# A two-layer trunk on one core: V product and last down product with tokens stationary, opening in halves, attention by token parity

## The chip, the core and the metric

The kernel runs on one core of one Trainium2 chip. The time is device microseconds of one execution, the median of several. Five engines work beside each other and meet at semaphores: TensorE (PE, with its weight loads listed apart as PEld), VectorE (DVE), ScalarE (ACT), GpSimd (POOL), and SyncE (SP), which here only issues DMAs.

## The reference

```python
# x: (1, 256, 2048) float32. Layer 0 mixes by gMLP, layer 1 by dilated attention; each is followed by a conv FFN.
h = h + gmlp_chunk_mixer(rms_norm(h, a_ln), ...)      # z = gelu(h W_in); u, v = split(z); v = layer_norm(v)
                                                      # mixed = tril(w_s) v per 128-token chunk + b_s; (u * mixed) W_out
h = h + conv_ffn(rms_norm(h, ffn_ln[0]), ...)         # (silu(dwconv3(h W_gate)) * (h W_up)) W_down, FFN_DIM 5632
h = h + dilated_attention_mixer(rms_norm(h, b_ln), ...)  # 3 groups x 8 heads, (window, dilation) = (128,1) (512,4) (2048,16)
h = h + conv_ffn(rms_norm(h, ffn_ln[1]), ...)
return rms_norm(h, final_ln)
```

With 256 tokens every window reaches back to the start, or nearly so: a query sees the keys of its group whose distance is no more than the window and a multiple of the dilation. For dilations 4 and 16 these have the parity of the query.

## The kernel before

Activations lie with features on the partitions: a tile of 128 features by 256 tokens. `h` is the residual (16 such tiles). Float32 accuracy comes out of float32r products by splitting: a weight tile W becomes `w_hi` (ACT copies `raw` and rounds) and `w_lo` (DVE subtracts), an activation becomes a high part and a low part that lie side by side in `X`, `GX`, `OX` or `hid` as 512 columns. For each 128 by 128 weight tile PE loads `w_hi`, streams the 512 columns, loads `w_lo` and streams the 256 high columns (`multiply`, L1054). The sum lands in two halves of a PSUM bank, which ACT and DVE add when they empty it.

All weights come as one stream of 784 units of 8 tiles (512 KB each). SP loads unit u into `raw[u % 4]` as soon as `w_lo` of unit u-4 is made (L341 on); ACT's and DVE's `split_step` (L439, L744) run two units ahead of the step they stand in; ACT may overwrite a slot when PE has finished the unit four back. Everything else that ACT and DVE do is written out by hand between these splits, by step number. The stages: V (units 0 to 31, from 10.41 us), U (32 to 63, from 103.71), AO (the gMLP's output product), F0 and D0 (FFN of layer 0), QKV (eight heads of 18 units, from 1030.64), WO, F1, and D1, the last down product (88 units, from 2011.60 to 2255.66).

What the change touches:

- **Opening.** SP issues `vecs`, then the four first units. ACT issues five loads of `x` (`X_LOADS`, blocks 2, 2, 4, 4, 4) and makes the high parts, DVE the low parts, each pair or four of them followed by one split. PE warms up with 30 matmuls on zeros. Then ACT squares `h` in pairs into `tsum` and `hc` in turn, and POOL adds them into `ssum` (L384); a square may only overwrite a tile that has been added. `mean_square` on PE sums over the partitions after unit 7.
- **V and U, layer norm.** V is emptied pair by pair (`scale_pair` on DVE, Gelu on ACT, L482), POOL sums the pairs into `vsum` (L398). The mean product (L1149) stands after unit 3 of U; then DVE subtracts the mean, ACT squares into U's last tiles, POOL adds eight times (L409), and after unit 10 PE waits for `ln_added` and takes the variance (L1154). From unit 14 on each feature tile is scaled (L925, L928), turned by PE (L1170), copied by ACT, and mixed by PE with `WS` (L1162); DVE adds the bias (`mix_bias`), POOL multiplies into U.
- **Attention.** `scores` (L1193) gives the first 128 queries 128 keys, the second 128 queries 256 keys, in each of three groups: 384 + 768 columns. `p_turn` turns nine 128 by 128 blocks, `attend` has nine products of 128 columns. These float32 products show as two PE instructions each; a turn shows as one.
- **End.** D1 is emptied as the other residual products are; `last_block` takes the last two tiles. Then PE turns `Y` (h times the final gain) to token-major in 32 turns (L1287) with the sum of squares between (L1304), ACT and DVE scale eight 128x512 pieces (L738, L1048), and SP stores them.

## Time and profile before

| | us |
|---|---|
| median of the timed runs | 2267.44 (2267.21 to 2267.46) |
| the profiled execution | 2269.09 |
| its span | 2267.4 |
| PE busy in the span | 2252.1 |
| DVE busy | 1479.9 |
| ACT busy | 1215.5 |
| POOL busy | 105.5 |

Busy time is time in which an engine has an instruction under way. A group of the page gives busy time, the mean duration of one, and the idle time of its engine before it with what ended that. A matmul's duration reaches past the start of the next one, because the array is pipelined; what counts in a stream is the distance from start to start. A timeline row gives a start, the time the row covers, and how many instructions were merged.

### The profile page before, as it was taken

Reading aid. Unit: us, or ns where it says so; the run is one execution under the profiler, and the core shown is the slowest. Engines: PE = TensorE matmul, PEld = TensorE weight load, DVE = VectorE, ACT = ScalarE, POOL = GpSimd, SP = SyncE. Lnnn points to the kernel's source line nnn. Section 1 sums busy time; section 2 is a strip of 40 time slices with the busy share of each in tenths; the row PEclk is TensorE's granted clock in tenths of the full one; section 3 lists DMA queues with packets and bytes.
Section 4 is the critical chain, followed back from the end, with each engine's and each line's share of the span. In section 5 each row is a group of like instructions: output and inputs, shape, how many; then the busy total and the mean of one; then the engine's idle time right before and its main releaser. Section 6 shows DMA issues by size and latency. Waiting matters only on the chain.

```text
span 2267.4 us, 37978 instructions
## 1 busy us (share of the span) xinstructions
PE 2252.1 (99%) x13098; PEld 1998.8 (88%) x13098; DVE 1479.9 (65%) x1764; ACT 1215.5 (54%) x1544; POOL 105.5 (5%) x85
## 2 busy tenths in 40 slices
PE   9999999999999999999999999999999999999998
PEld 7888888888888888888888888888888888888887
DVE  6577776767666655556666666687666666655453
ACT  6455566666666634445555555555555555544443
POOL 3122100000000000000000000020000000000000
PEclk9999999999999999999999999999999999999999
DMA  7645565555555565555555555556555555566564
GB/s 263 197 157 168 178 201 186 192 186 190 189 185 190 190 194 188 191 188 201 168 168 167 171 171 167 172 166 198 187 191 187 190 189 185 190 192 193 186 190 134
DMA packets 115478, 419.22 MB, mean 185 GB/s; under 512 B 12832, under 2 KB 12960, under 8 KB 115168
## 3 DMA queue, kind: packets, MB, share of 16 engines
q1 hardware_dynamic: 114192, 413.43, 56.3%
q0 software_dynamic: 512, 2.95, 0.3%
q10 hardware_dynamic: 720, 2.10, 0.2%
q8 instruction: 37, 0.61, 0.1%
q14 instruction: 17, 0.14, 0.0%
HBM read 416.33 MB, written 2.10 MB: 185 GB/s over the span
## 4 chain that ended last, share of the span: by engine, by line
PE 97%; POOL 1%; DMA 1%; DVE 0%; ACT 0%; issue 0%; ACTq 0%; DVEq 0%; POOLq 0%
PE acc L1063 61%; PE acc L1064 32%; POOL vsum L409 1%; DMA h<-x_t 1%; PE sc_ps L1218 0%; POOL ssum L384 0%; PE sc_ps L1198 0%; PE sc_ps L1205 0%; PE acc L1261 0%; PE sc_ps L1213 0%; PE sc_ps L1197 0%; PE misc L1189 0%; ACT U L618 0%; PE misc L1162 0%; PE sc_ps L1162 0%
## 5 line engine op out<-in xcount | busy, mean ns | idle before, releaser
L1063 PE MATMUL acc<-X,w_hi 128*128 128x512 f32 x4480 | 1564.3, 392 | 3.5 <-DVE w_lo L750 3.0
L750 DVE TENSOR_TENSOR w_lo<-raw,w_hi 128x1024 fp32r<-128x1024 f32 x784 | 967.9, 1241 | 527.5 <-ACT w_hi L446 527.2
L1064 PE MATMUL acc<-X,w_lo 128*128 128x256 f32 x4480 | 1263.3, 282 | 0.0
L446 ACT ACTIVATE w_hi<-raw 128x1024 fp32r<-128x1024 f32 x784 | 824.8, 1058 | 496.2 <-PE acc L1064 486.8
L1063 PEld LDWEIGHTS acc<-X,w_hi 128*128 128x128 f32 x4480 | 841.6, 188 | 179.6 <-DVE w_lo L750 3.6
L1064 PEld LDWEIGHTS acc<-X,w_lo 128*128 128x128 f32 x4480 | 847.2, 189 | 0.4
L1063 PE MATMUL acc<-hid,w_hi 128*128 128x512 f32 x1408 | 488.2, 390 | 0.0
L1064 PE MATMUL acc<-hid,w_lo 128*128 128x256 f32 x1408 | 397.1, 282 | 0.0
L1063 PEld LDWEIGHTS acc<-hid,w_hi 128*128 128x128 f32 x1408 | 264.4, 188 | 55.4
L1064 PEld LDWEIGHTS acc<-hid,w_lo 128*128 128x128 f32 x1408 | 266.1, 189 | 0.0
L456 ACT ACTIVATE hc<-acc 128x512 f32<-128x512 f32 x104 | 62.0, 596 | 157.3 <-PE acc L1064 157.3
L755 DVE TENSOR_TENSOR tsum<-hc,acc 128x512 f32<-128x512 f32 x104 | 71.5, 687 | 97.3 <-ACT hc L456 97.2
L374 POOL TENSOR_TENSOR ssum<-ssum,sq 128x512 f32<-128x512 f32 x24 | 33.0, 1376 | 1271.7 <-ACT sq L459 1271.7
L1063 PE MATMUL acc<-GX,w_hi 128*128 128x512 f32 x256 | 88.9, 391 | 0.0
L516 ACT ACTIVATE conv<-gu,vecs 128x256 f32<-128x256 f32 x88 | 53.1, 603 | 61.2 <-DVE gu L772 61.2
L772 DVE TENSOR_TENSOR gu<-tsum,rinv 128x512 f32<-128x512 f32 x104 | 72.3, 695 | 3.6
L1064 PE MATMUL acc<-GX,w_lo 128*128 128x256 f32 x256 | 72.2, 282 | 0.0
L654 ACT ACTIVATE hc<-acc 128x512 f32<-128x512 f32 (+1 forms) x40 | 22.2, 555 | 81.3 <-PE acc L1064 81.3
L466 ACT ACTIVATE X<-h,vecs (+1 forms) x48 | 22.0, 504 | 72.3 <-DVE h L786 71.9
L1063 PEld LDWEIGHTS acc<-GX,w_hi 128*128 128x128 f32 x256 | 48.0, 188 | 10.1
L766 DVE SCALAR_TENSOR_TENSOR X<-h,vecs,X (+1 forms) x64 | 38.5, 628 | 21.9 <-ACT X L466 17.7
L521 ACT ACTIVATE act_g<-conv 128x256 f32<-128x256 f32 x88 | 36.8, 419 | 26.7 <-DVE conv L801 26.5
(141 smaller groups left out, 1049.0 us busy)
## 6 DMA issues: line engine op xcount, KB each, us to landing
raw<-w_stream SPq DMA_DIRECT2D x784, 512.0 KB, 3.5
out<-out_sb SPq DMA_DIRECT2D x8, 256.0 KB, 2.9
h<-x_t ACTq DMA_DIRECT2D x3, 512.0 KB, 10.3
WS<-ws_t POOLq DMA_DIRECT2D x1, 1024.0 KB, 5.2
BS<-bs_row POOLq DMA_DIRECT2D x1, 1024.0 KB, 8.2
mask<-mask_d POOLq DMA_DIRECT2D x1, 576.0 KB, 4.0
h<-x_t ACTq DMA_DIRECT2D x2, 256.0 KB, 5.0
rope<-rope_d POOLq DMA_DIRECT2D x1, 256.0 KB, 3.2
```

What stands on the lines that cost most here:

```text
L374: nc.gpsimd.tensor_tensor(ssum[:, :], ssum[:, :], sq[:, :, :].rearrange("p a b -> p (a b)"), ALU.add).then_inc(ss_added, 1)
L409: nc.gpsimd.tensor_tensor(vsum[:, :, :], vsum[:, :, :], U[:, 12 + 2 * k:14 + 2 * k, :], ALU.add)\
L446: nc.scalar.activation(w_hi[slot][:, :], raw[slot][:, :], ACT.Copy).then_inc(hi_ready, 1)
L456: nc.scalar.activation(hc[:, :, :], acc[s][:, :, 0:S], ACT.Copy).then_inc(hcopied, 1)
L516: nc.scalar.activation(conv[:, :], gu[:, 0, 2:S + 2], ACT.Identity, bias=vecs[:, one(cv + 3 * FB + j)], scale=vecs[:, one(cv + 2 * FB + j) ...
L521: nc.scalar.activation(act_g[:, :], conv[:, :], ACT.Silu).then_inc(silued, 1)
L750: nc.vector.tensor_tensor(w_lo[slot][:, :], raw[slot][:, :], w_hi[slot][:, :], ALU.subtract)\
L755: nc.vector.tensor_tensor(tsum[:, :, :], hc[:, :, :], acc[s][:, :, S:2 * S], ALU.add)\
L766: nc.vector.scalar_tensor_tensor(X[:, 2 * pr + b, S:2 * S], h[:, 2 * pr + b, :], vecs[:, one(GAINS[n] + 2 * pr + b)], X[:, 2 * pr + b, 0:S ...
L772: nc.vector.tensor_tensor(gu[:, :, 2:S + 2], tsum[:, :, :], over(rinv, 2), ALU.mult)\
L1063: nc.tensor.matmul(bank, hi, moving[:, kt, :], start=first, stop=False)
L1064: op = nc.tensor.matmul(bank[:, S:2 * S], lo, moving[:, kt, 0:S], start=False, stop=last)
```

## The change

The stream, the split and all other stages stay.

- `token_unit` replaces `multiply` in V and D1. A unit is then two k-tiles by 512 output columns. For each k-tile and each half of the tokens PE loads the high part of the activations and streams 512 columns of `w_hi`, loads the low part and streams `w_hi`, loads the high part and streams `w_lo`: twelve matmuls of 512 columns in a unit, one PSUM bank for each 128 tokens.
- V lands token-major. `v_evac` applies the RMS factor and Gelu straight from PSUM and sums along the row; the layer norm's statistics are row sums on ACT (`v_square`) and DVE, its gain and bias come as broadcast rows (two further 1 MB loads on POOL's queue) and are applied by `v_norm`, two DVE instructions of 512 columns, eight times. POOL's sums, the two mean products and the turns of V go. The mixes move from after units 16 to 31 of U to after units 12 to 27. Two one-column products (`tok_ms`) join the first `mean_square`.
- The opening loads, rounds and splits the first unit in halves; `vecs` is loaded behind the first units; the warm-up has 15 matmuls; the split of a step now stands ahead of its two squares.
- Attention has the even tokens ahead of the odd ones. The groups with dilation 4 and 16 need keys of the same parity alone: 1024 score columns, eight turns, and in `attend` two products of 256 columns and four of 128.
- In D1 the last four units are run for the first 128 tokens and then for the others. `h` is turned to token-major beforehand, by 32 turns inside F1 (`h_turn`), so that the end needs none; the final norm's sum of squares is a row sum, the first half of the tokens is finished and stored apart from the second.

The opening loop stands on ACT, `v_norm` on DVE at steps 8 to 15 of U:

```diff
-        sp.dma_start(vecs[:, :], vecs_d).then_inc(vecs_landed, 16)
-        for slot in range(RING):
+        sp.dma_start(raw[0][:, 0:UC // 2], w_stream[0, :, 0:UC // 2]).then_inc(raw_half, 16)
+        sp.dma_start(raw[0][:, UC // 2:UC], w_stream[0, :, UC // 2:UC]).then_inc(raw_landed[0], 16)
+        for slot in range(1, RING):
             load(slot, 0, slot)
+        sp.dma_start(vecs[:, :], vecs_d).then_inc(vecs_landed, 16)
...
+        def token_unit(u, slot, pair_set, moving, k0, k_tiles, needs=None, half=None):
+            if half is None:
+                pe.wait_ge(lo_ready, u + 1)
+            for j in range(2):
...
+                hi, lo = w_hi[slot][:, COLS * j:COLS * (j + 1)], w_lo[slot][:, COLS * j:COLS * (j + 1)]
+                for t in range(2):
+                    bank = acc[pair_set][:, t, :]
+                    xh, xl = moving[:, kt, P * t:P * (t + 1)], moving[:, kt, S + P * t:S + P * (t + 1)]
+                    nc.tensor.matmul(bank, xh, hi, start=(kt == 0), stop=False)
+                    nc.tensor.matmul(bank, xl, hi, start=False, stop=False)
+                    op = nc.tensor.matmul(bank, xh, lo, start=False, stop=(kt == k_tiles - 1))
+            op.then_inc(units_done, 1)
...
-        for n, (tile, cols) in enumerate(((warm_r, 512),) * 16 + ((warm_r, P),) * 8 + ((warm_b, 512),) * 6):
+        for n, (tile, cols) in enumerate(((warm_r, 512),) * 11 + ((warm_r, P),) * 4):
...
+        for s in range(2, BLOCKS * BLOCK_UNITS + 4):
             split_step(U_V, s)
+            if s < 6:
+                for i in (2 * s - 4, 2 * s - 3):
+                    wait_pos(act, ss_added, i - 1)
+                    nc.scalar.activation((tsum, hc)[i % 2][:, :, :], h[:, pair_of(i), :], ACT.Square)\
+                        .then_inc(x_squared, 1)
...
+        def v_norm(c, t):
+            at = V[:, t, COLS * c:COLS * (c + 1)]
+            dve.wait_ge(ln_landed, 32)
+            nc.vector.scalar_tensor_tensor(at, at, v_shift[:, t:t + 1], ln_gain[:, COLS * c:COLS * (c + 1)],
+                                           ALU.add, ALU.mult).then_inc(v_gained, 1)
+            dve.wait_ge(v_gained, 2 * c + t + 1)
+            nc.vector.scalar_tensor_tensor(at, at, v_rinv[:, t:t + 1], ln_bias[:, COLS * c:COLS * (c + 1)],
+                                           ALU.mult, ALU.add).then_inc(v_normed, 1)
```

The lines of the diff on attention and on the end (the first `y_out` is ACT's; `h_turn` is PE's, after each of eight units of F1):

```diff
         def scores(h_, par):
             pe.wait_ge(roped, GROUPS * (h_ + 1))
             for g in range(GROUPS):
-                q, k = QK[par][:, g, 0, :], QK[par][:, g, 1, :]
-                nc.tensor.matmul(sc_flat[:, P * g:P * (g + 1)], q[:, 0:P], k[:, 0:P], start=True, stop=True)
-                op = nc.tensor.matmul(sc_flat[:, Q1 + S * g:Q1 + S * (g + 1)], q[:, P:S], k, start=True, stop=True)
+                for t in range(2):
+                    q = QK[par][:, g, 0, P * t:P * (t + 1)]
+                    a, b = (0, S) if g == 0 else (P * t, P * (t + 1))
+                    c = Q0 * t + (S + P * (g - 1) if g else 0)
+                    op = nc.tensor.matmul(sc_flat[:, c:c + b - a], q, QK[par][:, g, 1, a:b], start=True, stop=True)
...
+        def y_out(t):
+            act.wait_ge(y_biased, 1)
+            act.wait_ge(y_squared, 2 * BLOCKS - 1 + t)
+            nc.scalar.activation(fin_std[:, t:t + 1], y_rows[:, t, BLOCKS - 1:BLOCKS], ACT.Sqrt,
+                                 bias=y_bias[:, t:t + 1], scale=1.0 / D).then_inc(fin_rms[t], 1)
+            act.wait_ge(fin_rinv_ready[t], 1)
+            for c in (1, 2):
+                at = Z[:, t, COLS * c:COLS * (c + 1)]
+                nc.scalar.activation(at, at, ACT.Copy, scale=fin_rinv[:, t:t + 1]).then_inc(y_out_act[t], 1)
...
+        def h_turn(n):
+            wait_pos(pe, h_turned, n - 3)
+            for k in range(4):
+                op = nc.tensor.transpose(turned[n % 4][:, P * k:P * (k + 1)],
+                                         h[:, 2 * n + k // 2, P * (k % 2):P * (k % 2 + 1)], ident[:, :])
+            op.then_inc(h_to_turn, 1)
```

## Rows read from the trace of the kernel before

**Rows 1.** The page: the span and the busy time of each engine.

```profile
span 2267.4 us, 37978 instructions
PE 2252.1 (99%) x13098; PEld 1998.8 (88%) x13098; DVE 1479.9 (65%) x1764; ACT 1215.5 (54%) x1544; POOL 105.5 (5%) x85
```

**Rows 2.** PE's waits over the whole span: engine, line, releaser, us, times, longest.

```profile
PE misc L1154 <- POOL vsum L409: 2.0, 1, 2.0
```

**Rows 3.** Instructions grouped by line and shape: busy us, mean ns, then idle before.

```profile
L750 DVE TENSOR_TENSOR w_lo<-raw,w_hi 128x1024 fp32r<-128x1024 f32 x784 | 967.9, 1241 | 527.5 <-ACT w_hi L446 527.2
...
L446 ACT ACTIVATE w_hi<-raw 128x1024 fp32r<-128x1024 f32 x784 | 824.8, 1058 | 496.2 <-PE acc L1064 486.8 <-DMA raw<-w_stream 5.3 <-PE acc L1262 1.2
```

**Rows 4.** Stretches, one per stage: busy us of each engine, granted clock, DMA share, GB/s.

```profile
10.41:103.71 93.30, 90.34 (x519) 79.56 (x517) 61.81 (x61) 53.66 (x70) 26.45 (x18) 1.00 0.67 230
103.71:208.74 105.03, 102.99 (x619) 91.88 (x617) 78.66 (x105) 55.31 (x77) 31.20 (x18) 0.98 0.49 156
...
1030.64:1472.94 442.30, 442.30 (x2641) 395.14 (x2640) 301.88 (x362) 231.38 (x305) 3.48 (x5) 1.00 0.53 172
...
2011.60:2255.66 244.06, 244.06 (x1411) 216.37 (x1410) 118.56 (x107) 102.61 (x114) 9.82 (x8) 1.00 0.56 177
```

**Rows 5.** PE in order of time, in the last down product: start, duration, what.

```profile
2225.15 0.39 PE L1063 MATMUL acc<-hid,w_hi 128*128 128x512 f32 x1
2225.38 0.28 PE L1064 MATMUL acc<-hid,w_lo 128*128 128x256 f32 x1
2225.50 0.39 PE L1063 MATMUL acc<-hid,w_hi 128*128 128x512 f32 x1
```

**Rows 6.** PE in order of time, in the warm-up: start, duration of the group, count.

```profile
7.77 0.62 PE L1134 MATMUL acc<-warm_r 128*128 128x512 f32 x2
9.29 1.47 PE L1134 MATMUL acc<-warm_b 128*128 128x512 bf16 x6
```

**Rows 7.** PE in order of time, around the second mean product of the U stage.

```profile
137.28 1.98 PE L1154 MATMUL misc<-vsum,mean_w 128*128 128x256 f32 x4 [2.04 <-POOL vsum L409]
```

**Rows 8.** Two single units of the U stage, as stretches.

```profile
196.70:200.14 3.44, 3.44 (x23) 3.12 (x23) 3.36 (x6) 2.56 (x4) 0.00 (x0) 1.00 0.42 138
205.50:208.73 3.23, 3.23 (x23) 2.90 (x22) 1.93 (x4) 0.53 (x2) 2.61 (x2) 1.00 0.53 174
```

**Rows 9.** One DVE form at two lengths, grouped by line and shape.

```profile
L766 DVE SCALAR_TENSOR_TENSOR X<-h,vecs,X 128x256 fp32r<-128x256 f32 x20 | 8.5, 481 | 4.5 <-ACT X L580 3.4 <-ACT X L466 1.2
L983 DVE SCALAR_TENSOR_TENSOR sm<-sc_ps,mask 128x768 f32<-128x768 f32 x8 | 7.6, 947 | 0.0
```

**Rows 10.** The opening in order of time, on DVE, ACT and POOL.

```profile
7.76 1.23 DVE L750 TENSOR_TENSOR w_lo<-raw,w_hi 128x1024 fp32r<-128x1024 f32 x1 [1.47 <-ACT w_hi L446]
...
15.68 1.72 ACT L580 ACTIVATE X<-h,vecs 128x256 fp32r<-128x256 f32 x4 [0.19 <-DMA h<-x_t]
...
30.98 1.29 POOL L384 TENSOR_TENSOR ssum<-ssum,hc 128x512 f32<-128x512 f32 x1
```

**Rows 11.** The weight loads in 26 to 60 us: time from issue to landing.

```profile
DMA to landing us min/median/max: 3.1/3.4/8.0
```

**Rows 12.** PE in order of time, the attention products of one head.

```profile
1073.98 0.60 PE L1198 MATMUL sc_ps<-QK 128*128 128x256 f32 x2
1074.42 0.38 PE L1197 MATMUL sc_ps<-QK 128*128 128x128 f32 x2
1074.64 0.60 PE L1198 MATMUL sc_ps<-QK 128*128 128x256 f32 x2
...
1086.62 1.14 PE L1205 MATMUL sc_ps<-ident,sm 128*128 128x128 f32 x9
```

**Rows 13.** The end in time, on DVE, ACT and the SP queue.

```profile
2255.86 0.42 DVE L784 TENSOR_TENSOR tsum<-h,acc 128x256 f32<-128x256 f32 x1 [8.71 <-PE acc L1064]
...
2258.84 0.26 ACT L734 ACTIVATE fin_std<-acc,eps 128x2 f32<-128x2 f32 x1 [1.25 <-PE acc L1304]
...
2260.11 4.49 SPq L349 DMA_DIRECT2D out<-out_sb  x8
```

More of the change, by code:

```diff
@@ L538, in ffn @@
                             ffn_evac(1, p0 + c, c, stage, c, u0 + FIRST - 1 + c)
-                with act.Fori(layer, FB // 2) as i:
+                    for s in range(4, 12):
+                        c = s // 4 - 1
+                        split_step(u0 + FIRST, s)
+                        ffn_evac(1, p0 + 2 + c, 2 + c, s % 4, c, u0 + FIRST + 4 * (c + 1))
+                        for n in (0, 1) if s == 4 else (s - 3,):
+                            if n < NORM_PAIRS:
+                                h_turn(n)
+                with act.Fori(2 * layer, FB // 2) as i:
                     for s in range(4, 12):
@@ L555, in ffn, with last_down @@
                             down(i, s)
-                else:
-                    for s in range(4, 48):
-                        down(0, s)
-                    nc.scalar.activation(std[:, 0:1], eps[:, :], ACT.Sqrt).then_inc(rms_ready, 1)
-                    for s in range(4, 44):
-                        down(1, s)
-                        if s == 39:
-                            last_block(0)
-                    last_block(1)
+            def last_down():
+                for s in range(4, BLOCKS * LAST_UNITS):
+                    if U_D1 + s + AHEAD < UNITS:
+                        split_step(U_D1, s)
+                    if s % LAST_UNITS < 2 and s >= LAST_UNITS:
+                        y_square(s // LAST_UNITS - 1, s % LAST_UNITS)
+                nc.scalar.activation(tsum[:, 0, 0:1], eps[:, :], ACT.Sqrt).then_inc(rms_ready, 1)
+                for t in range(2):
+                    y_square(BLOCKS - 1, t)
+                    y_out(t)
+            act.dma_start(gain[:, :], gain_d).then_inc(gain_landed, 16)
             at = 0
@@ L1106, in pairs_by_depth, with product @@
                         mean_square(n)
-            def product(u0, p0, pairs, moving, k_tiles, needs, n=None, ms_at=3, deep=False):
+            def product(u0, p0, pairs, moving, k_tiles, needs, n=None, ms_at=3, deep=False, turn=None):
                 if deep:
@@ L1116, in product, with h_turn @@
                 per = 4 * k_tiles // UT
-                with pe.Fori(1, pairs // 2) as i:
+                if turn:
+                    two_pairs(u0 + per, p0 + 2, moving, k_tiles, None, turn)
+                with pe.Fori(2 if turn else 1, pairs // 2) as i:
                     two_pairs(u0 + per * i, p0 + 2 * i, moving, k_tiles)
+            def h_turn(n):
+                wait_pos(pe, h_turned, n - 3)
[3 more added lines that the diff above has]
+                op.then_inc(h_to_turn, 1)
@@ L1138, in _ @@
-            with pe.Fori(1, KT // 4) as i:
-                two_pairs(U_V + FIRST * i, P_V + 2 * i, X, KT)
+            for u in range(BLOCKS * BLOCK_UNITS):
+                c = u // BLOCK_UNITS
+                if c > 1 and u % BLOCK_UNITS == 0:
+                    pe.wait_ge(v_gelued, 2 * (c - 1))
+                token_unit(U_V + u, u % RING, c % 2, X, 2 * (u % BLOCK_UNITS), KT, normed_ready(0) if c == 0 else None,
+                           True if u == 0 else None)
+                if u == BLOCK_UNITS - 1:
+                    mean_square(0)
+                    for t in range(2):
+                        for b in range(2):
+                            op = nc.tensor.matmul(misc[:, S + t:S + t + 1], ssum[:, S * b + P * t:S * b + P * (t + 1)],
+                                                  mean_w[:, 0:1], start=(b == 0), stop=(b == 1))
+                    op.then_inc(tok_ms, 1)
```

597 lines of the change are left out of this document (316 added, 281 removed).

## The prediction

> **What bounds the kernel.** I read the page first: PE is busy for 99% of the span, DVE for 65% and ACT for 54% [rows 1]. So an edit counts by what it takes from PE's stream, or from what PE waits for. PE's waits come next; they are short, and the one that this change touches is 2.0 us on POOL's sums in the layer norm [rows 2]. The groups show what a unit of weights costs the others: 1.24 us on DVE and 1.06 on ACT [rows 3]. Last the stretches, one per stage [rows 4]. D1 is the cleanest: 244.06 us for 88 units, 2.77 a unit, 0.347 for each pair of matmuls. With 2.77 a unit as the measure, V (32 units, 88.6) has 4.7 us too much, U (88.6) has 16.4, QKV (144 units, 398.9) has 43.4. These excesses, the end, and the unit price itself are what the change can move.
>
> **The token-stationary unit.** Before, a unit is eight pairs; the distances from start to start are 0.23 for the 512 columns and 0.12 for the 256 [rows 5]. After, it is twelve matmuls of 512 columns. The columns are the same, 6144 in both. At 2.4 GHz they would take 2.56 us, so 0.21 of the 2.77 is spent at the sixteen changes from one matmul to the next, 0.013 each. If a change costs the same after either length, 512 columns take 0.227, and the unit 2.72. The warm-up has 512 columns after 512 columns in the same type: two cover 0.62 us, of which the last is 0.39, so 0.23 again [rows 6]. Twelve of exactly 0.23 are 2.76. I take 2.73, a gain of 0.04 per unit, 120 units: 4.8 us, of which 1.3 lie in V and 3.5 in D1. The bounds are far apart. Below, the bfloat16 warm-up rows, (1.47 - 0.38) / 5 = 0.218 each [rows 6], would make the unit 2.62 and the gain 18 us. Above, nothing in the trace has a split weight as the moving tile; I return to that as a rival. The stretch of ordinary units is the nearest in type and tile, so I stay by it.
>
> The Trainium skill ("TensorE: Matmul & The Clock Gate", section "Wait - 56ns, not 53.3ns?") gives a fixed 2.5 ns per warm matmul beyond its columns. By it, four matmuls fewer per unit would be worth 10 ns, 1.2 us in all instead of 4.8. The rows on float32r disagree, with some 13 ns per matmul, and I go by them.
>
> **Opening and V.** Now: `w_lo` of the first unit ends at 8.99 [rows 10], but PE is still in its warm-up and starts at 10.41 [rows 4]. The new warm-up is eleven 512-column matmuls at the 1.2 GHz level, 0.43 each by their columns, and four short ones: from 2.1 to about 7.7. The first half of `w_lo` should be there by then (one ACT issue of 0.5 more ahead of x, but half the load and half the instructions, and no `vecs` ahead). So PE starts 2.7 us earlier. That isn't the gain, since another chain ends later: the last x blocks are taken at 15.68 [rows 10], and the squares and POOL's eight adds end at 30.98 + 1.29 = 32.27 [rows 10]. The new order puts a split (1.06 of ACT [rows 3]) ahead of the first squares, so the adds end at about 33.0. PE has then run eight units from 7.7 (21.8) with some 3 us of waits for splits, and waits for the adds. Then `mean_square`, four instructions of 256 columns at 0.22 (a pair of them holds PE from 1073.98 to 1074.42 [rows 12]), 0.9, and `tok_ms`, eight instructions priced as 128-column ones, 0.11 each (1074.42 to 1074.64 for two [rows 12]), 0.9. Unit 8 starts at 34.8; 24 units of 2.73 end V at 100.3 instead of 103.7: 3.4 us gained, V's unit gain within it. Bounds: 1 (the splits now feel x more) to 5.
>
> Two more broadcast loads of 1 MB stand on POOL's queue, issued at about 33 to 35 us. Today a weight load beside two of them takes up to 8.0 us instead of 3.4 [rows 11]. With four, the slow time lasts longer, but each unit's split has about three units of lead (8.3 us), and loads for units up to 11 are issued before the adds end. I put 0.3 us of PE wait on it; 4 us if the queue holds weight loads back all the while.
>
> **U and the layer norm.** The excess of 16.4 is four things. The second mean product waits 2.04 for POOL and then its four instructions of 256 columns cover 1.98 [rows 7], some 0.43 each where 0.22 is usual: PE's clock fell to the 1.2 GHz level after the wait (0.98 for the stage [rows 4]). The turns: a unit with turn and mix takes 3.44, one with mix alone 3.23 [rows 8], 0.21 for 16 units. The mixes, 3.23 - 2.77 = 0.46 times 16 = 7.4, stay. All else goes: 16.4 - 7.4 = 9.0 us.
>
> What is late next? DVE. In the unit at 196.70 it is busy for 3.36 of 3.44 [rows 8]. From steps 8 to 15 it gets 16 `v_norm` instructions of 512 columns, two a step. Their price lies between 481 ns for 256 columns and 947 for 768 [rows 9], so 0.71; a step is 1.24 + 1.43 = 2.7, plus 1.4 in steps 8 and 12 for `scale_pair`, plus 0.42 for `mix_bias` from 13 on. Over eight steps that is 25.5 us against PE's 23.5. The backlog of 2 and the start (statistics done some 2.4 after step 8's data) fit into DVE's lead of about 6 us. I put 0.3 on it. The price if the cover fails is 1 us per unit for four or five units. POOL works against it: its gates (2.61 busy in the unit at 205.50 [rows 8]) would start while `v_norm` still runs. The Trainium skill ("SBUF - State Buffer", section "Who interferes with whom") says that a DVE instruction with two SBUF inputs and a GpSimd one that reads SBUF exclude each other for whole instructions; it speaks for rival (b). No row here shows such a collision by itself.
>
> **Attention.** Per head, start to start: 128-column instructions 0.11, 256-column ones 0.22 [rows 12]. Scores lose 128 of 1152 columns: 0.21. Turns: nine to eight, 0.11 (nine cover 1.14 with the last one's tail). `attend`: 18 instructions of 0.11 (2.0) become four of 0.22 and eight of 0.11 (1.76): 0.24. Together 0.56 a head, 4.5 us for eight. No wait is added; the strided writes of ACT and DVE stand where both have idle time (302 and 231 busy of 442 [rows 4]).
>
> **End.** `h_turn` adds 32 turns inside F1: 32 x 0.11 = 3.6 us lost, with ACT's eight copies in its idle time. At the end: today PE's last product leaves at 2255.66, DVE starts 0.2 later [rows 13], and the span ends 11.7 us after it. After: y_add at +0.2, 0.7 long; ACT's square with its accumulator read 0.8; root 0.3 (0.26 [rows 13]) and reciprocal 0.2; then two pieces each on ACT and DVE, the first out at +2.9. SP's eight stores take 4.49 [rows 13], 0.56 each; four of them from +2.9 on have the last issued at +4.6, and as today some 3.3 from the last issue to the end: +7.9. The first half of the tokens is finished behind the other half's 5.5 us of matmuls and costs nothing. Gain 3.8, bounds 3 to 5. D1's own gain is the 3.5 above.
>
> **The sum.** V and opening -3.4, U -9.0, attention -4.5, F1 +3.6, D1 -3.5, end -3.8, stalls +0.6: -20.0. The span of 2267.4 becomes 2247.4. The profiled execution lies 1.7 above its span, and the median of the timed runs, 2267.44, happens to lie at the span; I subtract from the median: 2247.4 us.
>
> **Rivals.**
> (a) The columns alone set PE's pace and the number of matmuls doesn't: the 4.8 falls away, 2252. For it: the columns are equal, and 0.23 as printed allows it. Against: 0.347 for 768 columns is more than they take.
> (b) DVE's burst in U or the four loads in V leave PE waiting after all: +3 to +7, and a wait of over 2 us would bring the clock down as at 137 us. About 2253.
> (c) The change doesn't do what it says in the opening: the adds end no earlier and PE waits as long. +3, 2250.5.
> (d) The slower side: a moving tile that ACT and DVE have just written, with a weight load ahead of every 512 columns, streams slower than the warm-up's zeros. The other parts bring 15.2 us; over 1440 matmuls that is 10.6 ns each, so it decides from 0.241 per matmul on. At 0.25 the unit is 3.0, D1 lasts 264, and the whole 2280. Against it: weight loads of the same kind already stand before every matmul and are hidden behind 256 columns.
> (e) They stream as the bfloat16 rows do: 2234.
>
> **Chances.** Forecast 0.58; (a) 0.13; (b) 0.13; (c) 0.06; (d) 0.05; (e) 0.05. The range 2240 to 2255 leaves out (d), (e) and the far end of (b). A measurement of this kernel tells 0.2% (4.5 us) from no change: faster 0.94, same 0.02, slower 0.04.
>
> **What would show it.** D1's 88 units at 240.2 us, start to start 0.2275; no turns or mean products in U, 98 us for the stage with the clock at full; unit 8 near 34.8; heads 0.56 shorter; 7.9 us after the last product. A D1 above 244 would make the forecast wrong, as would PE waits on `w_lo` in V or in U's units 10 to 18.

## The result

The changed kernel takes 2258.62 us (median; 2257.48 to 2258.96), the kernel before 2267.49 (2267.21 to 2269.21) beside it: ratio 0.9959, 95% interval 0.9949 to 0.9969. So it is faster, by 0.4%, less than half of what was forecast, and outside the range. The kernel before takes about 2267.5 us in some executions and about 2269.1 in others, so its median depends on the mix: the gain is 8.9 us by these medians and 10.4 by the profiled executions. Those took 2258.72 us after and 2269.09 before, each 1.7 to 1.8 above its span.

The profile after begins like the one before [rows 1]: the span is 10.5 us shorter, PE's busy time 10.7, and PE is still what bounds the kernel.

```profile
span 2256.9 us, 36477 instructions
PE 2241.4 (99%) x12503; PEld 1960.5 (87%) x12503; DVE 1454.6 (64%) x1732; ACT 1207.9 (54%) x1534; POOL 69.8 (3%) x61
```

The stages of the kernel after as stretches: V from the first matmul, V from its unit 8, U, QKV, F1, D1. The columns are those of [rows 4]: the busy us and count of PE, PEld, DVE, ACT and POOL, the granted clock, the DMA share and GB/s.

```profile
8.58:104.73 96.15, 94.09 (x397) 74.65 (x397) 52.25 (x51) 52.70 (x72) 18.65 (x13) 0.98 0.71 254
36.74:104.73 67.99, 67.64 (x291) 54.03 (x290) 32.60 (x28) 32.09 (x40) 3.31 (x2) 1.00 0.73 261
104.73:200.84 96.11, 96.11 (x578) 85.78 (x577) 72.63 (x88) 53.38 (x68) 14.06 (x8) 1.00 0.53 176
1022.63:1460.48 437.85, 437.85 (x2592) 390.57 (x2591) 299.17 (x362) 229.87 (x305) 3.44 (x5) 1.00 0.53 174
1509.03:2002.30 493.27, 492.78 (x2855) 436.93 (x2853) 342.22 (x443) 270.89 (x363) 2.82 (x2) 1.00 0.58 189
2002.30:2248.70 246.40, 246.40 (x1058) 198.21 (x1056) 116.31 (x109) 99.16 (x108) 0.57 (x1) 1.00 0.55 182
```

U, QKV and F1 came out as forecast. V and D1 did not: V ended at 104.73, later than before (103.71), and D1 took 246.40, longer than before (244.06). D1's PE rows in order of time show what is longer. The starts are 0.23 and 0.24 apart; over the stage they alternate and average 0.2333, so twelve are 2.80 us, where the eight pairs of before took 2.77.

```profile
2227.70 0.40 PE L1192 MATMUL acc<-w_hi,hid 128*128 128x512 f32 x1
2227.93 0.40 PE L1193 MATMUL acc<-w_hi,hid 128*128 128x512 f32 x1
2228.16 0.40 PE L1194 MATMUL acc<-w_lo,hid 128*128 128x512 f32 x1
2228.40 0.40 PE L1192 MATMUL acc<-w_hi,hid 128*128 128x512 f32 x1
```

The opening of the kernel after, in order of time, the ACT queue and ACT:

```profile
0.82 0.41 ACTq L643 DMA_DIRECT2D gain<-gain_d  x1
1.26 2.93 ACTq L646 DMA_DIRECT2D h<-x_t  x5
...
6.17 0.91 ACT L656 ACTIVATE X<-h,gain 128x256 fp32r<-128x256 f32 x2 [0.45 <-DMA h<-x_t]
...
9.39 0.91 ACT L656 ACTIVATE X<-h,gain 128x256 fp32r<-128x256 f32 x2 [1.27 <-DMA h<-x_t]
...
11.96 1.71 ACT L656 ACTIVATE X<-h,gain 128x256 fp32r<-128x256 f32 x4 [0.71 <-DMA h<-x_t]
...
17.07 1.70 ACT L656 ACTIVATE X<-h,gain 128x256 fp32r<-128x256 f32 x4
18.68 1.04 ACT L482 ACTIVATE w_hi<-raw 128x1024 fp32r<-128x1024 f32 x1
```

ACT waits for x three times; before, the last x blocks were taken at 15.68 [rows 10], now at 17.07. POOL's eight adds begin later by that 1.4 and by the split that the new order puts ahead of the squares, and they end at 33.62 + 1.29 = 34.91 instead of 32.27 [rows 10]:

```profile
20.40 2.07 POOL L442 TENSOR_TENSOR ssum<-ssum,tsum 128x512 f32<-128x512 f32 x1 [18.17 <-ACT tsum L670]
...
33.62 1.29 POOL L442 TENSOR_TENSOR ssum<-ssum,hc 128x512 f32<-128x512 f32 x1
```

PE has a late start of its own. It waits 1.92 us for the first `w_lo` and starts at 8.58. In the 3.4 us before that it was busy for 1.55, and then its granted clock was at the 1.2 GHz level for 3.4 us: the starts from 9.15 to 11.71 are 0.43 apart instead of 0.2333, and the first unit takes 4.39 us instead of 2.80. Before, the clock stayed at full from 7.7 us until behind the wait at 137 us.

```profile
5.11:8.52 3.41, 1.55 (x9) 1.19 (x8) 1.72 (x4) 2.54 (x6) 0.00 (x0) 1.00 0.98 324
8.52:11.93 3.41, 3.35 (x8) 2.71 (x9) 1.94 (x4) 1.86 (x3) 0.00 (x0) 0.50 1.02 418
```

So two chains meet ahead of unit 8: the sums, done at 34.91, and PE's own first eight units. PE's row there shows how close they are, a wait of 0.39 us:

```profile
34.96 1.13 PE L1213 MATMUL misc<-ssum,mean_w 128*128 128x256 f32 x4 [0.39 <-POOL ssum L442]
```

### The profile page after: what moved, and what is told of

Its sections match the earlier page's. It is cut to its first block, busy times and chain, and to the rows that moved or that the text cites. A ratio compares the mean times of both kernels' runs of the same rounds, so it can differ in the third digit from the quotient of the medians.

```text
span 2256.9 us, 36477 instructions
## 1 busy us (share of the span) xinstructions
PE 2241.4 (99%) x12503; PEld 1960.5 (87%) x12503; DVE 1454.6 (64%) x1732; ACT 1207.9 (54%) x1534; POOL 69.8 (3%) x61
## 4 chain that ended last, share of the span: by engine, by line
PE 97%; DMA 1%; POOL 1%; DVE 1%; ACT 0%; issue 0%; ACTq 0%; DVEq 0%; POOLq 0%; SPq 0%
PE acc L1168 53%; PE acc L1169 28%; PE acc L1192 4%; PE acc L1193 4%; PE acc L1194 4%; PE sc_ps L1362 1%; DMA raw<-w_stream 1%; POOL ssum L442 1%; DMA h<-x_t 0%; PE sc_ps L1381 0%; DVE w_lo L814 0%; PE sc_ps L1369 0%; PE sc_ps L1378 0%; PE acc L1425 0%; PE misc L1351 0%
## 5 line engine op out<-in xcount | busy, mean ns | idle before, releaser
L1168 PE MATMUL acc<-X,w_hi 128*128 128x512 f32 x4224 | 1473.4, 391 | 0.5 <-DVE h L855 0.5
L1169 PE MATMUL acc<-X,w_lo 128*128 128x256 f32 x4224 | 1190.8, 282 | 0.0
L1168 PE MATMUL acc<-hid,w_hi 128*128 128x512 f32 x704 | 244.1, 390 | 0.0
L1169 PE MATMUL acc<-hid,w_lo 128*128 128x256 f32 x704 | 198.5, 282 | 0.0
L1168 PEld LDWEIGHTS acc<-hid,w_hi 128*128 128x128 f32 x704 | 132.2, 188 | 27.7
L1169 PEld LDWEIGHTS acc<-hid,w_lo 128*128 128x128 f32 x704 | 133.1, 189 | 0.0
L1194 PE MATMUL acc<-w_lo,hid 128*128 128x512 f32 x336 | 132.9, 396 | 0.0
L1192 PE MATMUL acc<-w_hi,hid 128*128 128x512 f32 x336 | 132.9, 396 | 0.0
L1193 PE MATMUL acc<-w_hi,hid 128*128 128x512 f32 x336 | 132.9, 395 | 0.0
L1168 PE MATMUL acc<-GX,w_hi 128*128 128x512 f32 x256 | 88.8, 390 | 0.0
L1192 PEld LDWEIGHTS acc<-w_hi,hid 128*128 128x128 f32 x336 | 63.1, 188 | 15.4
L1194 PEld LDWEIGHTS acc<-w_lo,hid 128*128 128x128 f32 x336 | 63.1, 188 | 15.3
L1193 PEld LDWEIGHTS acc<-w_hi,hid 128*128 128x128 f32 x336 | 63.1, 188 | 15.1
## 6 DMA issues: line engine op xcount, KB each, us to landing
ln_gain<-ln_row POOLq DMA_DIRECT2D x1, 1024.0 KB, 11.9
ln_bias<-ln_row POOLq DMA_DIRECT2D x1, 1024.0 KB, 15.1
```

Of the source, the lines that this page charges most:

```text
L1168: nc.tensor.matmul(bank, hi, moving[:, kt, :], start=first, stop=False)
L1169: op = nc.tensor.matmul(bank[:, S:2 * S], lo, moving[:, kt, 0:S], start=False, stop=last)
L1192: nc.tensor.matmul(bank, xh, hi, start=(kt == 0), stop=False)
L1193: nc.tensor.matmul(bank, xl, hi, start=False, stop=False)
L1194: op = nc.tensor.matmul(bank, xh, lo, start=False, stop=(kt == k_tiles - 1))
```

## The experiments

Two things had to be explained: 0.07 us too much on each of the 120 token-stationary units, and V's late start and long middle. My first theory for the units was the address at which the streamed tile lies. In this kernel the split weights start on a multiple of 2048 bytes, and X, the hidden tile and the other tiles of the arena 32 bytes past one (`SKEW = 32`). In the feature-stationary products the second kind is streamed, in the token-stationary ones the first. The rival was rival (d) in a mild form: freshly split weights stream slower wherever they lie.

**Moving both kinds.** The weights' tiles go behind the arena at an offset of their own, and `SKEW` varies:

```diff
-SKEW = 32
+SKEW = 0          # a_x0_w0, a_x0_w32; 32 in a_w32 and a_w96
+W_SKEW = 0        # 32 in a_w32 and a_x0_w32, 96 in a_w96
-        w_hi = [sb(f"w_hi{i}", [P, UC], F32R) for i in range(RING)]
-        w_lo = [sb(f"w_lo{i}", [P, UC], F32R) for i in range(RING)]
+        w_at = nc.sbuf_base + (KT + FB) * row + W_SKEW
+        w_hi = [nc.alloc_sbuf_tensor_at(f"w_hi{i}", [P, UC], F32R, offset=w_at + 4 * UC * i) for i in range(RING)]
+        w_lo = [nc.alloc_sbuf_tensor_at(f"w_lo{i}", [P, UC], F32R, offset=w_at + 4 * UC * (RING + i)) for i in range(RING)]
```

Expected of `a_w32`:

> The changed kernel with the split weights moved so that they start 32 bytes past a 2048-byte line of SBUF, as the activations do; nothing else moves. Address theory: a 512-column stream is slow when the moving tile starts on the line, and fast 32 bytes past it; the token unit falls from 2.80 to 2.73 us, D1 from 246.4 to 240.2, the kernel by some 8 us to about 2250.5. Role theory (a split weight as the moving operand, freshly written, is slow wherever it lies): 2.80, 2258.6.

Expected of `a_x0_w0`:

> The changed kernel with activations and split weights both on a 2048-byte line. Address theory: the token units stay at 2.80, and the feature units slow down too, by some 7 ns for each 512 columns and up to as much for the 256: 664 units of 8 pairs, 37 to 74 us more, 2296 to 2333. Role theory: no change, 2258.6. If the address of the stationary operand is what counts, the token units get faster and the others stay.

Expected of `a_x0_w32`:

> The changed kernel with the activations on a 2048-byte line and the split weights 32 bytes past one: the reverse of the kernel as it was given. Address of the moving operand: token units fast (2.73), feature units slow, 2288 to 2325. Only the distance between the two operands counts: both as in the given kernel, 2258.6. Role theory: 2258.6.

Expected of `a_w96`:

> As the run with the weights at 32 bytes, but at 96, so that they are 64 bytes past the activations. If the conflict repeats every 64 bytes, token units take 2.72 and the feature stages are slow as there, about 2276; if only an equal place on the 2048-byte line counts, token units take 2.80 and feature units 2.77, about 2258.6.

Measured: 2276.43 us (2275.02 to 2276.95), 2278.69 (2277.16 to 2279.23) and 2281.56 (2280.81 to 2292.07), ratios to before 1.0034, 1.0042 and 1.007, and for `a_w96` 2286.16 in a single execution. What the two kinds of product cost, from the PE rows in order of time (X and weights in bytes past a 2048-byte line; `a_skew64` and `a_hid0` are told below):

| kernel | X, arena | weights | token matmul, us | D1, us | feature pair in F0, us |
|---|---|---|---|---|---|
| after | 32 | 0 | 0.2333 | 246.2 | 0.3467 |
| a_w32 | 32 | 32 | 0.2267 | 239.2 | 0.3533 |
| a_x0_w0 | 0 | 0 | 0.2267 | 239.2 | 0.3533 |
| a_x0_w32 | 0 | 32 | 0.2333 | 246.2 | 0.3533 |
| a_w96 | 32 | 96 | 0.229 | 241.5 | 0.3533 |

(D1 here is from the first matmul's start to the last one's; a token matmul is a 1055th of that.) The address theory falls: with the weights at 0 a token matmul costs 0.2333 in one kernel and 0.2267 in another. So does the rival, for the same fresh weights stream at 0.2267. What the token-stationary prices go with is the distance between the two operands' places: in V and in D1 they are lowest, of these kernels, where it is zero. `a_w96` lies between, at 2.75 a unit, where my expectation had 2.72 or 2.80.

A feature-stationary pair has two prices as well, 0.0066 apart. In F0 and D0 it is cheap only where the streamed tile is 32 bytes past the stationary one. F0, D0 and F1 have 3520 pairs, which is 23 us against the 7 won in D1 and the 1 or 2 won in V, so moving everything loses 18 us or more. (U and QKV lose less by it, 0.7 and 2.0 us in `a_w32`, the gMLP's output product AO nothing there.) The first stretch of `a_x0_w0` is F0, 9.4 longer than the 488.97 of before and after, the second D1.

```profile
289.99:788.34 498.35, 498.35 (x2822) 432.18 (x2821) 339.86 (x439) 323.28 (x397) 1.82 (x2) 1.00 0.56 186
2029.87:2269.29 239.42, 239.42 (x1058) 198.01 (x1056) 116.11 (x109) 99.08 (x108) 0.57 (x1) 1.00 0.59 187
```

But the distance alone does not settle the price of a feature-stationary pair. In `a_x0_w32` F0 (first row) is dear, while F1 (second row) costs 493.20, as little as the 493.27 of the changed kernel, though its X and its weights lie in the same tiles as F0's; in `a_w32` F1 takes 501.8. And AO, with distance zero in both, takes 88.8 us in `a_w32` and 89.9 in `a_x0_w0`. What else counts for these pairs stays open.

```profile
291.00:789.34 498.34, 498.34 (x2822) 432.78 (x2821) 339.84 (x439) 323.54 (x397) 1.81 (x2) 1.00 0.57 186
1532.62:2025.82 493.20, 493.20 (x2855) 433.49 (x2853) 341.54 (x442) 271.05 (x362) 2.09 (x2) 1.00 0.57 189
```

**The hidden tile of layer 1 alone.** The four kernels above moved many tiles at once. By this reading it is enough for D1 to move the one tile that is stationary there:

```diff
+        hid_last = nc.alloc_sbuf_tensor_at("hid_last", [P, FB, 2 * S], F32R, offset=arena_at + 2016)
```

ACT and DVE write it in layer 1 and D1 reads it, in place of `hid`. The distance to the weights is 0; in the other kernels the 2016 is 32, 96, 224, 480 or 992, for a distance of 64, 128, 256, 512 or 1024 bytes. (All but the one at 64 also make the region 2016 bytes longer, which moves the small tiles behind it.)

Expected of `a_hid0`:

> The changed kernel with only the second layer's hidden tile moved, to the same place on a 2048-byte line as the split weights; all stages with features stationary keep their 32 bytes of distance. If the distance between the stationary tile and the moving one sets the price, D1 falls from 246.2 to 239.2 us and nothing else moves: the kernel at 2251.6. If the cheap token units of the earlier run came from where the weights lay, D1 stays at 246.2: 2258.6.

Expected of `a_hid64`:

> As the run with the moved hidden tile, but 64 bytes past the line. Distance repeating every 64 bytes: D1 at 239.2 and the kernel at 2251.6. Otherwise D1 at 246.2 and 2258.6.

Expected of `a_hid128`:

> The changed kernel with layer 1's hidden tile 128 bytes past the weights' place in the 2048-byte line. If only distance zero is good, the last down product takes 246.2 us and the kernel 2258.6. If the step is 128 bytes, 239.2 and 2251.5.

Expected of `a_hid256`:

> The changed kernel with layer 1's hidden tile 256 bytes past the weights' place. If the grid is 512 bytes, 256 is as far off it as can be, and by the row at 128 (between) the price is that or higher: 245 to 246.2 us for the last down product, 2256 to 2258.6 in all. If the grid is 256 bytes: 239.2 and 2251.5.

Expected of `a_hid512`:

> The same with 512 bytes, the length of one stationary block of 128 columns. If only distance zero in the 2048-byte line is good: 246.2 us and 2258.6. If what counts is that both tiles' blocks begin on one 512-byte grid: 239.2 and 2251.5. I hold the second the likelier, since the four stationary blocks of a row themselves stand at 0, 512, 1024 and 1536 and are all at the low price when the tile is at distance zero.

Expected of `a_hid1024`:

> The same with 1024 bytes, half a line. As for 512 bytes: 239.2 us and 2251.5 if a grid of 512 or 1024 bytes is what counts, 246.2 and 2258.6 if the whole line does.

Measured: `a_hid0` 2251.48 us (2251.16 to 2252.23), ratio 0.9925 (0.9907 to 0.9942), 7.1 less than the changed kernel by an edit of one address. PE in D1 of `a_hid0`, where the starts are 0.22 and 0.23 apart, and the stretch:

```profile
2219.72 0.39 PE L1194 MATMUL acc<-w_hi,hid_last 128*128 128x512 f32 x1
2219.95 0.39 PE L1195 MATMUL acc<-w_hi,hid_last 128*128 128x512 f32 x1
2220.17 0.39 PE L1196 MATMUL acc<-w_lo,hid_last 128*128 128x512 f32 x1
2220.40 0.39 PE L1194 MATMUL acc<-w_hi,hid_last 128*128 128x512 f32 x1
```

```profile
2002.11:2241.50 239.39, 239.39 (x1058) 198.08 (x1056) 116.15 (x109) 99.03 (x108) 0.57 (x1) 1.00 0.57 187
```

The other distances, a single execution each: 64 bytes 2257.66 us, 128 bytes 2256.37, 256 bytes 2250.70, 512 bytes 2251.33, 1024 bytes 2250.71. D1 as a stretch, for 128 and for 256 bytes:

```profile
2001.02:2246.40 245.38, 245.38 (x1058) 198.76 (x1056) 116.26 (x109) 99.12 (x108) 0.57 (x1) 1.00 0.57 183
```

```profile
2001.38:2240.76 239.38, 239.38 (x1058) 198.02 (x1056) 116.12 (x109) 99.03 (x108) 0.57 (x1) 1.00 0.58 187
```

512 and 1024 bytes give 239.39 and 239.38. (The whole times differ by more than D1 does, because the opening varies; see the gain load.) The kernel at 128 bytes has the longer region too and its D1 is slow, so the region's length is not the cause. So it is not the place in the 2048-byte line, as I had it after the first kernels, nor the grid of 512 bytes that I then held likelier: 256, 512 and 1024 bytes are as good as 0, while 32, 64 and 128 are not (246.4, 246.4, 245.4). At 128 bytes neither side of my expectation came out: 245.4 is a little less than the dear 246.4. These distances fit a grid of 256 bytes for the token-stationary matmuls. What in the chip makes it so isn't shown.

**The other kind at 64 bytes.** `a_hid0`'s hidden tile on the line, X and the arena 64 bytes past it:

```diff
-SKEW = 32
+SKEW = 64
```

> The kernel with layer 1's hidden tile at the weights' place (2251.5 us), and X and the arena (GX, OX, layer 0's hidden tile) 64 bytes past the weights' place instead of 32. The last down product stays at 239.2 either way. If a pair of feature-stationary matmuls is low at any distance that is not on the weights' place and ahead of it: 347 ns a pair, 2251.5 in all. If only 32 bytes is: 353 ns, 6.6 more for each of about 5300 pairs, so 2286; AO's products, whose moving tile kept its price before, stay at 88.8.

Measured 2284.24 us in a single execution; F0 498.33, as long as at distance 0, and D1 239.41. AO went up too, from 88.8 to 90.5, which neither side expected. So 32 bytes was the one distance tried at which a feature-stationary pair of F0 is cheap, and at that distance the token-stationary matmuls are dear.

**The gain load.** In the opening, what is new ahead of x is the 128 x 16 load of `gain`, issued by ACT first. `a_gain_pool` has POOL issue it, `a_gain2` has ACT issue it behind the first x load:

```diff
-            act.dma_start(gain[:, :], gain_d).then_inc(gain_landed, 16)
+            pool.dma_start(gain[:, :], gain_d).then_inc(gain_landed, 16)   # a_gain_pool, ahead of the memsets
+                if load == 0:                                               # a_gain2, in the loop over X_LOADS
+                    act.dma_start(gain[:, :], gain_d).then_inc(gain_landed, 16)
```

Expected of `a_gain_pool`:

> The changed kernel with the small gain load issued by POOL instead of by ACT ahead of x. If that issue is what delays x, the x loads land 0.45 us earlier, and the end of POOL's adds moves from 34.9 back by 0.5 to 1; the kernel gains 0.5 to 1, about 2258. If x is late because the raw units no longer stand behind the large vector load, nothing moves: 2258.6.

Expected of `a_gain2`:

> The changed kernel with the small gain load issued by ACT behind the first x load instead of ahead of it. With the gain on POOL's queue, ACT waited for the gain to land until 6.9, but the adds still ended 1.4 us sooner. If what costs is the issue time ahead of x, ACT starts on x at about 5 and the adds end at 32.5 to 33.5: 2256 to 2257. If the small load itself holds up the x loads behind it, only the first comes sooner and the adds end near 34.9 as in the changed kernel: 2258.6.

Measured: 2257.04 us (2256.88 to 2257.4) and 2257.38 (2256.97 to 2257.51), 1.6 and 1.2 less than the changed kernel, ratios to before 0.9949 (0.9932 to 0.9966) and 0.9949 (0.9932 to 0.9967). ACT in the opening of `a_gain_pool`: it starts x 0.7 later, since the gain now lands last, but never waits for x again behind that.

```profile
6.88 0.91 ACT L656 ACTIVATE X<-h,gain 128x256 fp32r<-128x256 f32 x2 [2.13 <-DMA gain<-gain_d]
...
8.74 0.89 ACT L656 ACTIVATE X<-h,gain 128x256 fp32r<-128x256 f32 x2
9.54 1.04 ACT L483 ACTIVATE w_hi<-raw 128x1024 fp32r<-128x1024 f32 x1
10.49 1.69 ACT L656 ACTIVATE X<-h,gain 128x256 fp32r<-128x256 f32 x4
...
15.59 1.70 ACT L656 ACTIVATE X<-h,gain 128x256 fp32r<-128x256 f32 x4
```

The last x blocks are at 15.59, POOL's adds end at 33.57, unit 8 starts at 35.41 instead of 36.74. In `a_gain2`, where one x load is ahead of the gain and four behind it, the x waits are 0.18, 0.80 and 0.66, and unit 8 starts at 35.77.

One trace of the opening says less than this seems to. Eleven kernels here (the six `a_hid` ones, `a_skew64` and the four that move both kinds) have the opening code of the changed kernel and take the last x blocks at 16.08 to 17.43 and unit 8 at 35.73 to 37.09. The four kernels with the gain on POOL (`a_gain_pool` and three told below) take them at 15.44 to 15.59 and at 35.30 to 35.41, outside that range, and none of them waits for x behind the gain. So the gain load on ACT's queue does cost, 1.1 us (`a_pool_hid` against `a_hid0`) to 1.6 by the medians. `a_gain2` lies within the range of the unchanged opening, so its trace does not show which place on ACT's queue matters; only its timed runs (2256.97 to 2257.51, for 2257.48 to 2258.96) speak for a gain.

**The opening in halves, undone.** One load, one `w_hi`, one `w_lo` and one wait for the first unit (`raw_half`, `hi_half`, `lo_half` gone):

```diff
-            sp.dma_start(raw[0][:, 0:UC // 2], w_stream[0, :, 0:UC // 2]).then_inc(raw_half, 16)
-            sp.dma_start(raw[0][:, UC // 2:UC], w_stream[0, :, UC // 2:UC]).then_inc(raw_landed[0], 16)
+            sp.dma_start(raw[0][:, :], w_stream[0, :, :]).then_inc(raw_landed[0], 16)
```

> The changed kernel with its first unit whole: one load of raw tile 0, one w_hi, one w_lo, one wait. My theory: the halves bring the first matmul forward, but unit 8 still waits for POOL's last square sum, which comes from the x loads and ACT's X steps; so the first matmul comes 0.5 to 1.2 us later, unit 8 stays at 36.6 to 36.9 and the time at 2258.6 (2258.2 to 2259.0). Rival, the prediction's reading in which the opening in halves carries a part of the gain: unit 8 is later by the half unit that PE lost, about 0.7 us: 2259.3.

Measured 2258.66 us (2258.58 to 2258.74), the changed kernel's time. PE and POOL of this kernel: the first matmul comes 2.3 later than in the changed kernel, more than either side had, and POOL's last add ends where it did, at 34.81. But PE does not wait for it: unit 7's last matmul starts at 35.29 and `mean_square` follows at once.

```profile
10.85 0.76 PE L1185 MATMUL acc<-w_hi,X 128*128 128x512 f32 x1 [4.03 <-DVE w_lo L974]
...
35.29 0.39 PE L1187 MATMUL acc<-w_lo,X 128*128 128x512 f32 x1
35.52 1.02 PE L1206 MATMUL misc<-ssum,mean_w 128*128 128x256 f32 x4
```

```profile
33.52 1.29 POOL L441 TENSOR_TENSOR ssum<-ssum,hc 128x512 f32<-128x512 f32 x1
```

So my theory was wrong on unit 8. It starts at 37.19, 0.45 later than the 36.74 of the changed kernel and outside the 36.6 to 36.9 that I expected, because here PE's own units are the later chain. Of the 2.3 us of the first matmul 0.45 are left at unit 8; the rest PE makes up, since the changed kernel waits 1.32 us for `w_lo` ahead of unit 6 and 0.39 for the sums, and this one for neither. The equal times come from behind unit 8: from there to V's end this kernel takes 67.37 us and the changed one 67.99, so V ends at 104.56 and 104.73. That the halves are worth nothing is not shown; what they save is less than what one opening differs from the next.

**The row loads in V.** ACT's waits between 36 and 105 us in the changed kernel, and then in one that issues `ln_gain` and `ln_bias` only when 16 units are done:

```profile
ACT w_hi L482 <- DMA raw<-w_stream: 8.2, 6, 2.4
```

```profile
ACT w_hi L483 <- DMA raw<-w_stream: 1.8, 2, 1.7
```

```diff
...                                           # the two loads stood ahead of the mask
+            pool.wait_ge(units_done, 16)     # behind POOL's mask of WS
             pool.dma_start(ln_gain[:, :], ln_row[0:1, :].partition_broadcast(P)).then_inc(ln_landed, 16)
             pool.dma_start(ln_bias[:, :], ln_row[1:2, :].partition_broadcast(P)).then_inc(ln_landed, 16)
```

> The changed kernel with POOL's two row loads ln_gain and ln_bias (landing after 11.9 and 15.1 us, beside the weight loads) issued only once 16 units of V are done. Theory: these two loads take the weight loads' share of the DMA engines, and this is the 0.6 to 0.7 us by which unit 13 of V is long. Issued later they make the same wait later, as the ring of raw tiles is as tight there: unit 13 goes to 2.8 to 3.1 us and a later unit (19 to 22) is long instead, time unchanged 2258.6. Rival: with only these two, and not WS and BS beside them, the weight loads keep up: no long unit, 2257.9.

Measured 2257.73 us (2257.28 to 2258.37). From unit 8 to V's end it is 67.29 us instead of 67.99, with no long unit, and the median is 0.9 lower, though the two kernels' times overlap. My theory said that the wait would only move, and it did not. That the row loads are the cause this pair does not show: `a_whole`, which loads them early, has no long unit either (67.37). The firmer pair is `a_best` and `a_best_ln` below, 66.62 and 65.43 us over these units, with times that do not overlap.

**Together.** `a_pool_hid` is `a_hid0` with the gain on POOL. `a_best` adds X of layer 0 in a tile `X0` at `x_at - SKEW`, on the weights' line, for V and U. `a_best_ln` adds the late row loads.

```diff
+        X0 = nc.alloc_sbuf_tensor_at("X0", [P, KT, 2 * S], F32R, offset=x_at - SKEW)
```

Expected of `a_pool_hid`:

> The changed kernel with two edits at once: layer 1's hidden tile at the weights' place in the 2048-byte line (alone 7.1 us less than the changed kernel), and the gain load issued by POOL (alone 1.6 us less). If the two causes are independent, as I hold, their gains add: 2258.6 - 7.1 - 1.6 = 2249.9 us, with unit 8 near 35.4 and the last down product at 239.2 us. Rival: the gain load's 1.6 us was a matter of what else is laid out or loaded, and is not there again: 2251.5.

Expected of `a_best`:

> As the run before it of this call, and the opening's X (V and U products) also at the weights' place in the line, in a tile of its own name that starts 32 bytes lower; from layer 0's attention on, X is where it was. By the rows of the two kernels with both at one place: a token unit of V 2.72 us for 2.80 (24 units that follow each other at TensorE's pace: -1.9, less where the opening's waits set the pace, so -1.3), the U products' pair of matmuls 353 ns for 347 (32 units: +0.7). Sum -0.6 to -1.2: 2249.0 us (2248.6 to 2249.4). Rival: it is not the place in the line but which of the two roles a fresh tile has, in which case V stays at 2.80 and the time is 2249.9 or above.

Expected of `a_best_ln`:

> The best version so far (hidden tile of layer 1 and the opening's X at the weights' place in the line, gain load issued by POOL: 2249.3 us), and the two row loads ln_gain and ln_bias issued once 16 units of V are done. Alone that took away the long unit of V, 0.7 us. If the causes are independent: the unit of 3.69 us goes to 2.7 to 2.9, time 2248.5 (2248.2 to 2248.9). Rival: with a faster V the weight loads are late by themselves, and the time stays at 2249.3.

Measured: 2250.39 us (2250.11 to 2250.52), 2249.34 (2249.1 to 2249.52) and 2248.26 (2248.16 to 2248.78); ratios to before 0.9918 (0.9902 to 0.9935), 0.9914 (0.9897 to 0.993) and 0.9913 (0.9896 to 0.9929). The causes add up to within 0.5. `a_best_ln` from unit 8 to V's end, and its D1:

```profile
35.38:100.81 65.43, 65.43 (x291) 54.16 (x290) 34.41 (x28) 31.86 (x40) 3.08 (x3) 1.00 0.76 271
1998.97:2238.35 239.38, 239.38 (x1058) 198.01 (x1056) 116.14 (x109) 99.03 (x108) 0.56 (x1) 1.00 0.58 187
```

The 65.43 for 24 units is 2.73 each, V ends at 100.81 (the forecast had 100.3), and the whole is 2248.3: with two tiles moved, the gain load issued by POOL and the two row loads later, the kernel is about where the prediction had put it.

## Where the prediction was right and wrong

**The unit: wrong.** The step that failed was "I take 2.73", by what the stream's and the warm-up's rows show. Measured: 2.80, above the 2.77 of the eight pairs, so the gain of 0.04 a unit was a loss of 0.03. D1 went from 244.06 to 246.40 (+2.3 for -3.5), and V's 24 units behind unit 8 paid 24 x 0.07 = 1.7. Counting was not the mistake: in a layout that suits it the same unit takes 2.72, which is the price worked out from 0.013 per change of matmul. The mistake was to take [rows 5] and [rows 6] as prices of an instruction, when they are prices of an instruction with its operands at given places. The warm-up's stationary and streamed operands start at one place (`warm_r` is both), and the starts from 7.77 to 8.45 us are 0.227 apart, the price found at distance zero. The change swapped the operands' roles in a layout set for the old ones. The distance may not be all that counts: the changed kernel's warm-up, at one place too, has its starts 0.231 apart at the full clock (5.18 to 6.10 us), which is not explained. The bounds named only columns, types and freshness; the nearest rival, (d), had the right place and the wrong mechanism, and at 0.2333 stayed below the 0.241 from which it would have decided.

The Trainium skill ("TensorE: Matmul & The Clock Gate", section "Step-by-step: what each phase is for") says that two independent read ports feed the streamed operand and the weight loads, so that loading the next weights takes no SBUF read bandwidth from the running matmul. The runs show that this is not enough to price a matmul: in D1, with the same columns and the same loads, the time from start to start is 0.2267 or 0.2333 by the place of the stationary tile alone. Whether it is the two reads that meet there, they don't show.

**V and the opening: wrong, 4.4 us.** The step "the adds end at about 33.0" counted the split ahead of the squares, and left out the gain load's effect on x. Adds ended at 34.91: 0.95 from the split, 1.4 from x, 0.3 from a longer first add. (Of the 1.4, a part may be how one opening differs from the next.) From there the working held: 34.91 + 1.8 is 36.74, as 33.0 + 1.8 was 34.8. That was in part luck, for PE's own chain was as late: it started at 8.58 for 7.7, and no term had the 1.6 us by which the first unit is long at the lower clock behind the wait for `w_lo`, nor the 0.07 on each unit. PE waited only 0.39 for the sums, and only 0.15 in `a_gain_pool`, where they are done at 33.57. "No `vecs` ahead" counted what the change takes from the start and not the small load that it puts on the queue of the x loads. Behind unit 8 come the units' 1.7, and 0.7 for the wait for weights, for which the forecast had 0.3 among its stalls. The prediction said of PE's early start that another chain ends later. That is so, but by 0.39 us only: where PE loses more than that, unit 8 moves, as `a_whole` shows.

The longer first add has a cause that the rows show, the collision that the prediction named and found in no row. POOL's add takes 1.29 us where no split runs beside it and 2.07 to 2.09 where DVE's `w_lo` was under way; a split that starts beside an add takes up to 2.3 instead of 1.22, and it is this one that PE waits for at 28.71.

```profile
24.85 1.30 POOL L442 TENSOR_TENSOR ssum<-ssum,tsum 128x512 f32<-128x512 f32 x1
26.35 2.30 DVE L814 TENSOR_TENSOR w_lo<-raw,w_hi 128x1024 fp32r<-128x1024 f32 x1 [2.80 <-ACT w_hi L482]
27.71 2.09 POOL L442 TENSOR_TENSOR ssum<-ssum,tsum 128x512 f32<-128x512 f32 x1
```

**U: right.** 105.03 to 96.11, -8.9 for -9.0, and the clock at full. (The "98 us for the stage" among the signs did not follow from the sum, which gives 96.0.) The rival of DVE's burst did not come, though the collision did: beside POOL's first gate, at 149.63, a `v_norm` instruction took 1.78 us instead of 0.74. In two units with `v_norm` (stretches, columns as above) DVE is busy for 3.07 of 3.14 and 3.19 of 3.23, and PE waits for nothing in the stage.

```profile
137.96:141.10 3.14, 3.14 (x21) 2.83 (x20) 3.07 (x5) 1.55 (x2) 0.00 (x0) 1.00 0.55 167
141.10:144.33 3.23, 3.23 (x22) 2.90 (x21) 3.19 (x5) 1.64 (x3) 0.00 (x0) 1.00 0.49 162
```

**Attention: right.** 442.30 [rows 4] to 437.85 for QKV, -4.5 as forecast; the output product behind it, 48.92 to 48.55, gave 0.4 more that no term had. **F1: right.** 489.75 to 493.27, +3.5 for +3.6.

**End: nearly right.** The half of the tokens that finishes last goes as worked out: DVE 0.2 after the last product leaves (2248.70), the first output pieces 2.3 behind it and 0.7 long.

```profile
2248.90 0.69 DVE L917 TENSOR_TENSOR h<-acc,h 128x512 f32<-128x512 f32 x1 [2.38 <-PE acc L1282]
2249.62 0.63 ACT L558 ACTIVATE y_junk<-h 128x512 f32<-128x512 f32 x1 [2.92 <-DVE h L917]
...
2250.96 1.34 ACT L570 ACTIVATE Z<-Z,fin_rinv 128x512 f32<-128x512 f32 x2 [0.23 <-DVE fin_rinv L930]
```

The span ends 8.2 after the last product for 7.9, against 11.7 before: -3.5 for -3.8.

**The base.** I subtracted from the median of the three times shown, 2267.44, though the profiled execution took 2269.09, and the kernel before gave medians of 2268.9 to 2269.1 beside the later experiments. That step alone made the forecast 1.7 too low. On the spans the terms give -10.5 for -20.0: 5.8 of the 9.5 missing are D1's, 4.4 V's, the rest cancels. With the base's 1.7 that is the whole distance of 11.2. D1's 5.8 and the 1.7 of V's units, 7.5 together, are the unit's price, and the experiments show that cause; the rest of V's 4.4 is read from single traces and is less firm.

## What to carry to other kernels

A matmul's price holds for the places of its two operands: when a change swaps which is stationary and which is streamed, the offset between them needs tuning again, and it can be done for one tile at a time (here one address was worth 7.1 us). A small load put ahead on a queue whose loads feed the path can delay them; try it on a queue that has nothing due. An earlier start is worth no more than the distance to the next chain that gates the same units, so price both chains: here they were 0.39 us apart. And when a stretch is compared between kernels, look first at how much it differs among kernels that have the same code there.

## What was not expected of the hardware

- The distance between the stationary and the streamed operand changes the time from start to start of float32r matmuls: 0.2267 us (distance 0, 256, 512, 1024 bytes) or 0.2333 (32, 64; D1 at 128 is 1.0 less than at these) for 512 columns behind 512 with the tokens stationary (0.229 with the weights 64 ahead). In F0 it is 0.3467 (32) or 0.3533 (0, 64, and the weights ahead by 32 or 64) for a pair of 512 and 256 columns with the features stationary; F1 has 0.3467 in one kernel whose F0 has 0.3533. Neither that nor why the two kinds want different distances is explained.
- The 8 KB gain load ahead of five x loads on ACT's queue goes with waits of ACT for x of 0.45, 1.27 and 0.71 us; with it on POOL's queue, in four kernels, there are none behind the gain.
- Two broadcast loads of 1 MB, landing after 11.9 and 15.1 us beside the weight loads, cost V up to 1.2 us (`a_best` against `a_best_ln`, 66.62 and 65.43); issued once 16 units are done, they left no long unit.
- POOL's add and DVE's `w_lo` subtraction, both with two inputs in SBUF, lengthen each other when they overlap: 2.09 us instead of 1.29, and up to 2.3 instead of 1.22.
